# A two-layer diffusion step on one core: P.V by query, one-operation map combination, and early half chunks of the output projection

## What is computed

```python
s = einsum('bqhsd,bkhsd->bshqk', q, k) * scale     # two maps, s = 0, 1
p = softmax(s, axis=-1)
a = p[:, 0] - lam * p[:, 1]
o = einsum('bhqk,bkhe->bqhe', a, v)
o = o * rsqrt(mean(o * o, axis=-1) + 1e-6)         # norm of each query's 128 values of a head
o = o * subln_g * (1.0 - lam_init)
out = concatenate([att, conv], axis=-1) @ w_out
```

## Time and profile before

| | us |
|---|---|
| median of 3 runs | 2104.5 (2101.49 to 2108.45) |
| profiled execution | 2101.44 |
| its span, first to last instruction | 2099.7 |
| PE busy (matmuls) | 1942.6, 93% |
| VectorE busy | 1074.2, 51% |
| ScalarE busy | 811.3, 39% |
| mean granted TensorE clock | 0.959 of 2.4 GHz |

### The profile page before, as it was taken

How to read it: one execution, slowest core, us unless ns; L and a number is a source line. 1 busy time by engine, 2 the same in 40 slices (tenths; PEclk the granted TensorE clock), 3 DMA queues, 4 the chain that set the end, 5 groups by cost and what they waited for, 6 DMA issues and landing times. The chain is left out here.

```text
span 2099.7 us, 29845 instructions
## 1 busy us (share of the span) xinstructions
PE 1942.6 (93%) x12261; PEld 1758.1 (84%) x12261; DVE 1074.2 (51%) x1617; ACT 811.3 (39%) x1316; POOL 114.6 (5%) x93
## 2 busy tenths in 40 slices
PE   5699988989999999989998888699999999999895
PEld 2699956979999999989997578598898998989784
DVE  1542475542322232236326744476676766867574
ACT  3321165242211222233213632465565555655452
POOL 1000000100000000010000001020000000002201
PEclk7899999989999999989999998799999999999997
DMA  8315300322322242304251001366676666768551
GB/s 312 130 72 201 110 1 1 111 85 106 121 73 108 91 177 67 119 31 160 82 201 51 1 11 51 122 219 220 216 243 210 221 220 213 245 210 281 191 179 52
DMA packets 84817, 289.56 MB, mean 138 GB/s; under 512 B 10661, under 2 KB 14117, under 8 KB 84673
## 3 DMA queue, kind: packets, MB, share of 16 engines
q1 hardware_dynamic: 78192, 270.14, 36.9%
q0 software_dynamic: 6480, 17.43, 2.5%
HBM read 281.12 MB, written 12.26 MB: 140 GB/s over the span
## 5 line engine op out<-in xcount | busy, mean ns | idle before, releaser
L1477 DVE TENSOR_TENSOR w_lo<-raw,w_hi 128x1024 fp32r<-128x1024 f32 x396 | 490.6, 1241 | 436.0 <-ACT w_hi L1057 423.2
L1057 ACT ACTIVATE w_hi<-raw 128x1024 fp32r<-128x1024 f32 x396 | 417.2, 1054 | 378.9 <-PE ps L603 179.0
L603 PE MATMUL ps<-a_hi,w_hi 128*128 128x320 f32 x1728 | 403.0, 315 | 30.2 <-DVE w_lo L1477 15.8
L603 PE MATMUL ps<-a_lo,w_hi 128*128 128x320 f32 x1728 | 397.6, 312 | 0.0
L901 PE MATMUL ps<-hg,w_hi 128*128 128x416 f32 x1232 | 386.1, 370 | 12.1 <-DVE w_lo L1477 10.0
L603 PE MATMUL ps<-a_hi,w_lo 128*128 128x320 f32 x1728 | 397.3, 311 | 0.0
L603 PEld LDWEIGHTS ps<-a_hi,w_hi 128*128 128x128 f32 x1728 | 292.2, 191 | 47.6 <-issue 30.6
L902 PE MATMUL ps<-hg,w_lo 128*128 128x208 f32 x1232 | 320.7, 260 | 0.0
L603 PEld LDWEIGHTS ps<-a_lo,w_hi 128*128 128x128 f32 x1728 | 293.2, 190 | 0.0
L603 PEld LDWEIGHTS ps<-a_hi,w_lo 128*128 128x128 f32 x1728 | 292.4, 190 | 0.0
L901 PEld LDWEIGHTS ps<-hg,w_hi 128*128 128x128 f32 x1232 | 234.9, 191 | 15.7 <-DVE w_lo L1477 10.8
(11 more groups left out here) (209 smaller groups left out, 2089.2 us busy)
## 6 DMA issues: line engine op xcount, KB each, us to landing
raw<-gu_w SPq DMA_DIRECT2D x222, 512.0 KB, 4.3
raw<-moe_down_w SPq DMA_DIRECT2D x88, 512.0 KB, 4.4
ada_raw<-ada_w SPq DMA_DIRECT2D x21, 2048.0 KB, 8.0
raw<-in_w SPq DMA_DIRECT2D x48, 512.0 KB, 10.0
raw<-down_w SPq DMA_DIRECT2D x22, 512.0 KB, 3.4
raw<-out_w SPq DMA_DIRECT2D x16, 512.0 KB, 3.5
ada_pro<-ada_w SPq DMA_DIRECT2D x3, 2048.0 KB, 17.6
y_rows<-ey POOLq DMA_DIRECT2D x7, 512.0 KB, 4.1
```

What stands on the lines that cost most here:

```text
L603: ins = nc.tensor.matmul(out[:, hf, 0:HALF], w, o[:, hf * HALF:(hf + 1) * HALF], start=f, stop=e)
L1057: nc.scalar.activation(w_hi[:, s, :], raw[:, n % RAW, :], ACT.Copy).then_inc(hi_done, 1)
L1477: nc.vector.tensor_tensor(w_lo[:, s, :], raw[:, n % RAW, :], w_hi[:, s, :].bitcast(F32), ALU.subtract)\
```

## The change

1. PV by query: the transposed map is the weights, the values move, so an output block has the 128 queries on the partitions and the head's features along the row. VectorE copies it to `att` (`take_output`), at the head of step i for step i-2.
2. Maps combined in one operation: the first map isn't normalised any more. A one-column operation makes `cmix` = -lambda x (row sum 0) / (row sum 1), and one operation makes map 0 + cmix x map 1. The head norm takes the scale out again; its epsilon is multiplied by the square of row sum 0 (`reps`).
3. ScalarE's order in a step: exponential, tail copy, exponential, head copy. Heads 0 to 2 are squared within the steps 7, 12 and 17, and VectorE sums them along the row in steps 8, 13 and 18.
4. The norm per query: sums of squares plus `reps`, root, reciprocal, and a multiplication of each head by its queries' factors (`scale_head`). PE then transposes each head (five blocks) into PSUM blocks 3 and 0 in turn; ScalarE writes the high part with the gain as its scale, VectorE the low part, both from PSUM.
5. The convolution half of output chunk 0 runs in step 19 ahead of its transposes, that of chunk 1 after the last weighing of the values; the head blocks of both follow head by head. Block numbers are padded (`PAD`) so that the two chunks get blocks 1 and 2.
6. The router's small tables move to memory of the expert stage.

```diff
-                 ("sub", 0, 2 * HEADS, 1), ("out", OUT_CH, OUT_CH, OUT_CH), ("norm2", 0, 2, 1)]
+                 ("sub", 0, HEADS, None), ("out", OUT_CH, OUT_CH, OUT_CH), ("norm2", 0, 2, 1)]
...
+            if dg is None:
+
+                dg = (1 - g) % 4
+                PAD[l] = dg
...
-                two_blocks([(n0, g0), (n0 + 1, g0 + 1)], opnd, order, HEADS, KB)
...
-                        ins = nc.tensor.matmul(OT[:, i % 2, :], vtok[:, k0 // P + j, h * VH:(h + 1) * VH],
-                                               pT[:, i % 2, j * P:(j + 1) * P], start=(j == 0), stop=(j == nk // P - 1))
+                        ins = nc.tensor.matmul(OT[:, i % 2, :], pT[:, i % 2, j * P:(j + 1) * P],
+                                               vtok[:, k0 // P + j, h * VH:(h + 1) * VH],
+                                               start=(j == 0), stop=(j == nk // P - 1))
...
+                def first_chunks(cs_, j0, j1):
+
+                    for j in range(j0, j1):
+                        k = order[j]
+                        pe.wait_ge(alo_done, operand[l, "cat"] + j + 1)
+                        for c in cs_:
+                            ins = product(ps[:, (og0 + c) % 4], ((on0 + c) % SPLIT, k), a_hi[:, k, :], a_lo[:, k, :],
+                                          j == 0, j == KB - 1)
+                            if j == KB - 1:
+                                ins.then_inc(mm_done, 1)
...
+                    if i == NS - 1:
+
+                        pe.wait_ge(exp_done, 2 * (l + 1) * NS - 2)
+                        pe.wait_ge(lo_done, on0 + 1)
+                        first_chunks([0], 0, HEADS)
                     pe.wait_ge(comb_done, l * NS + i + 1)
...
                 pe.wait_ge(exp_done, 2 * (l + 1) * NS)
+                pe.wait_ge(lo_done, on0 + 2)
+                first_chunks([1], 0, HEADS)
                 for h in range(HEADS):
-                    pe.wait_ge(att_sq, HEADS * l + h + 1)
-                    sums_of(g0, TT * h, [sq[:, h % 2, :]])
-                    if h % 2:
-                        two_blocks(first, operand[l, "cat"], order, h - 1, h + 1)
-                for h in range(HEADS):
-
-                    pe.wait_ge(att_diag, HEADS * l + h + 1)
+
+                    pe.wait_ge(att_norm, HEADS * l + h + 1)
                     if h >= 2:
-                        pe.wait_ge(att_norm, HEADS * l + h - 1)
-                    spread(g0 + 3 * (h % 2), sq[:, h % 2, :])
+                        pe.wait_ge(alo_done, operand[l, "cat"] + HEADS + h - 1)
+                    flat = ps[:, (3, 0)[h % 2]].rearrange("p b c -> p (b c)")
+                    for t in range(TT):
+                        ins = nc.tensor.transpose(flat[:, t * P:(t + 1) * P], att[:, h, t * P:(t + 1) * P], idn[:])
+                    ins.then_inc(mm_done, 1)
+                    if h:
+                        first_chunks([0, 1], HEADS + h - 1, HEADS + h)
+                first_chunks([0, 1], KB - 1, KB)
...
                 for i in range(NS):
                     exponentials(2 * i)
                     if i >= 1:
+                        take_tail(i - 1)
+                    exponentials(2 * i + 1)
+                    if i >= 1:
                         take_transposed(i - 1)
-                    exponentials(2 * i + 1)
-                    if i >= 2:
-                        take_output(i - 2)
...
+                    if i % 5 == 2 and i > 5:
+                        square_head(i // 5 - 1)
+
+                nc.scalar.activation(warm[:], eps[:], ACT.Sqrt)
+                take_tail(NS - 1)
                 take_transposed(NS - 1)
...
+                square_head(HEADS - 1)
+                act.wait_ge(att_ms, l + 1)
+                nc.scalar.activation(rms[:], ssq[:], ACT.Sqrt, scale=1.0 / VH).then_inc(att_root, 1)
                 for h in range(HEADS):
-                    act.wait_ge(att_norm, HEADS * l + h + 1)
-                    nc.scalar.activation(a_hi[:, h, :], att[:, h, :], ACT.Copy).then_inc(ahi_done, 1)
+                    act.wait_ge(mm_done, q0 + h + 1)
+                    flat = ps[:, (3, 0)[h % 2]].rearrange("p b c -> p (b c)")
+                    nc.scalar.activation(a_hi[:, h, :], flat[:, 0:T], ACT.Copy, scale=subgs[:, l:l + 1])\
+                        .then_inc(ahi_done, 1)
...
+                def take_output(i):
+                    h, t, _, _ = STEPS[i]
+                    dve.wait_ge(pv_done, l * NS + i + 1)
+                    nc.vector.tensor_copy(att[:, h, t * P:(t + 1) * P], OT[:, i % 2, :]).then_inc(att_ready, 1)
+
+                def sum_head(h):
+                    dve.wait_ge(att_sq, HEADS * l + h + 1)
+                    nc.vector.tensor_reduce(ssq[:, h, :], sq[:, h % 2, :].rearrange("p (t c) -> p t c", c=VH), AX, ALU.add)\
+                        .then_inc(att_sum, 1)
...
+                    if i >= 2:
+                        take_output(i - 2)
                     dve.wait_ge(exp_done, 2 * (l * NS + i + 1))
 
-                    link(nc.vector.reciprocal(rinv[:, b, :], rsum[:, b, :]))
-                    link(nc.vector.tensor_scalar(pr[:, b, 1, 0:nk], pr[:, b, 1, 0:nk], rinv[:, b, 1:2], nlam[:, 0:1],
-                                                 ALU.mult, ALU.mult))
-                    nc.vector.scalar_tensor_tensor(pr[:, b, 0, 0:nk], pr[:, b, 0, 0:nk], rinv[:, b, 0:1],
-                                                   pr[:, b, 1, 0:nk], op0=ALU.mult, op1=ALU.add)\
+                    link(nc.vector.reciprocal(rinv[:, b:b + 1], rsum[:, h, t, 1:2]))
+                    link(nc.vector.scalar_tensor_tensor(cmix[:, b:b + 1], rinv[:, b:b + 1], nlam[:, 0:1],
+                                                        rsum[:, h, t, 0:1], op0=ALU.mult, op1=ALU.mult))
+                    nc.vector.scalar_tensor_tensor(pr[:, b, 0, 0:nk], pr[:, b, 1, 0:nk], cmix[:, b:b + 1],
+                                                   pr[:, b, 0, 0:nk], op0=ALU.mult, op1=ALU.add)\
                         .then_inc(comb_done, 1)
...
+                    if i % 5 == 3 and i > 5:
+                        sum_head(i // 5 - 1)
+
+                link(nc.vector.scalar_tensor_tensor(reps[:], rsum[:, :, :, 0], EPS * VH, rsum[:, :, :, 0],
+                                                    op0=ALU.mult, op1=ALU.mult))
+                take_output(NS - 2)
+                take_output(NS - 1)
+                sum_head(HEADS - 1)
+                dve.wait_ge(att_sum, HEADS * (l + 1))
+                nc.vector.tensor_tensor(ssq[:], ssq[:], reps[:], ALU.add).then_inc(att_ms, 1)
...
+                scale_head(0)
+                for h in range(HEADS):
+                    if h + 1 < HEADS:
+                        scale_head(h + 1)
+                    dve.wait_ge(ahi_done, operand[l, "cat"] + HEADS + h + 1)
+                    flat = ps[:, (3, 0)[h % 2]].rearrange("p b c -> p (b c)")
+                    nc.vector.scalar_tensor_tensor(a_lo[:, h, :], flat[:, 0:T], subgs[:, l:l + 1],
+                                                   a_hi[:, h, :].bitcast(F32), op0=ALU.mult, op1=ALU.subtract)\
+                        .then_inc(alo_done, 1)
```

More of the change, by code:

```diff
@@ L190 @@
 DENSE_BLOCKS = blocks_of(DENSE)
+PAD = {}
 def plan():
@@ L285, in hybrid_step @@
         nbias = sb("nbias", [P, 4])
-        rsum = sb("rsum", [P, 2, 2])
-        rinv = sb("rinv", [P, 2, 2])
+        rsum = sb("rsum", [P, HEADS, TT, 2])
+        rinv = sb("rinv", [P, 2])
+        cmix = sb("cmix", [P, 2])
+        ssq = sb("ssq", [P, HEADS, TT])
+        reps = sb("reps", [P, HEADS, TT])
+        warm = sb("warm", [P, 1])
         wr = sb("wr", [P, KB, EXPERTS])
@@ L357, in hybrid_step @@
             ey_lo = sb("ey_lo", [P, ST, D], F32R, c=moe)
+            gates = sb("gates", [P, TT, EXPERTS], c=moe)
+            oh = sb("oh", [P, 2, TT, EXPERTS], c=moe)
+            mask = sb("mask", [P, TT, EXPERTS], c=moe)
+            before = sb("before", [P, TT + 1, EXPERTS], c=moe)
+            rank = sb("rank", [P, TT, EXPERTS + 1], c=moe)
+            grouped = sb("grouped", [P, TT, EXPERTS, 2], F32R, c=moe)
+            logits = sb("logits", [P, TT, EXPERTS], c=moe)
+            tv = sb("tv", [P, TT, 8], c=moe)
+            ti = sb("ti", [P, TT, 8], U32, c=moe)
+            tf = sb("tf", [P, TT, 8], c=moe)
         ht_hi = a_hi[:].rearrange("p a b -> p (a b)").rearrange("p (t d) -> p t d", t=TT)
@@ L391, in hybrid_step @@
         diag_ready = sem("diag_ready")
-        att_diag = sem("att_diag")
+        att_sum = sem("att_sum")
+        att_ms = sem("att_ms")
         xn_done = sem("xn_done")
@@ L770, in turn_weights @@
                     ins.then_inc(done, 1)
+                on0, oq0, og0 = AT[l, "out"]
+                order = [4, 5, 6, 7, 0, 1, 2, 3]
+                def first_chunks(cs_, j0, j1):
[7 more added lines that the diff above has]
+                                ins.then_inc(mm_done, 1)
                 scores(0, 1)
@@ L1180, in take_transposed, with square_head @@
                         .then_inc(pt_ready, 1)
```

(31 more changed lines are left out.)

41 lines of the change are left out of this document (5 added, 36 removed).

## The result

The kernel after takes 2064.93 us (median of 4 runs, 2062.37 to 2067.44) against 2102.99 for the kernel before, measured beside it (2101.31 to 2108.45): ratio 0.9819, 95% interval 0.9804 to 0.9834. That is 38 us less. The forecast was 26 less, and its range ended at 2068: right in sign, too small by 12 us, and outside the range. (Against 2078.5 the miss is 13.6; the other 1.5 is the median of before, 2104.5 when the forecast was made.)

The account below looks back on a forecast made before the run. A loop of waits through three engines bounds the attention step at 4.41 us. Gains of 5.6 + 7.4 = 13.0 a layer, 26 in all, take 2101.4 to 2075.4; the median's 3.1 more gives 2078.5 us, range 2070 to 2086.

Parts of the forecast that it names:

- The loop of the step: Full attention step: PV, output copy on VectorE, reciprocal, small operation, combination, transposes, next PV; 4.30 us, before 4.41.
- PE alone: Full attention step: PE's own work from PV through scores and transposes to the next PV, 4.06 us.
- At PV of step 17: Attention steps up to the start of PV of step 17: 5.6 us per layer saved.
- The end: From the start of PV 17 to the end of output chunks 0 and 1: 25.0 against 32.4, 7.4 us per layer saved.
- The clock: Single stretches at 1.2 GHz: as many as before; none would give back some 5 us, twice as many cost as much.
- rival (d): Attention steps: fuller steps keep the clock up and PE alone bounds them, another 8 us at most, 2070; chance 0.08.
- (6): Shorter PV operands, padded block numbers and small tables placed in the expert stage's memory: counted as nothing.
- (a): Full steps: the output copy holds VectorE's path for 0.6 us, steps take 4.7, time 2088; chance 0.12.
- (b): End of attention: chunk 0's early half delays step 19's transposes, some 2 us a layer, 2082; chance 0.07.
- (c): PV in some 17 steps per layer: exposed weight loads add 0.12 us each, 4 us in all, 2082; chance 0.05.
- (e): Attention steps: head copy behind a late second exponential delays transposes and PV; slower, 2115 at 5.2 a step; chance 0.04.
- (f): In front of output chunk 2: the saved idle time comes back there, so no gain, 2104; chance 0.03.

Follow-up runs that it names:

- filler kernel: The kernel before with matmuls repeated in PE's gaps around the short step, the result unchanged: 2101.1 us, ratio 0.9974 (0.9960 to 0.9988).

## Why the prediction fell short, and what it had right

- **The loop of the step**, forecast 4.30 us, the copy taken at 0.20: measured 4.34 and 0.21. The five gaps of a head were to be 4.44, 4.31, 4.31, 4.05 and 3.40; the trace has 4.42, 4.34, 4.34, 3.95 and 3.40, in all 20.45 for 20.5. That the output copy would be late next, with PE alone right under it, is shown from both sides: twice, it adds 0.33 to a step; away from VectorE, PE alone bounds it. PE alone is 3.99, not 4.06: from scores to transposes 1.49 (1170.10 to 1171.59) where I had taken the idle time off 1.91 and kept 1.56.
- **At PV of step 17**, 5.6 us per layer: from the stage's beginning it took 84.0 us in layer 0 before and 77.3 after, 6.7, of which 1.1 is the one half-clock stretch that went: 5.6.
- **The end**, 7.4 us per layer: from that PV to the end of chunk 1 24.2 us for a forecast 25.0, so 8.2. Most terms are close: up to PV of step 19 7.9 for 8.1, from the head transposes to the first product 2.57 for 2.65, that wait 1.07 within the 1 to 2 named. Most of the 0.8 is in the head products with the transposes between them, 8.44 (353.86 to 362.3) for 7.04 + 1.84, since a set of five transposes holds the products up by 0.46 (355.72 to 356.18) and not by the 0.92 I took.
- Together a stage without clock effects was to give 13.0 and gave 13.9. That is 1.8 us of the miss. In the profiled executions, 39.1 us apart, the miss is 13.1: these 1.8, the clock's 6.3, and 4.9 outside the stages.
- **The clock** is the step that failed: "I take as many as before". Five stretches became none in the stages of after, 6.3 us, about half of the miss. I had seen that PE was busy for 0.83 of 2 us ahead of a fall, and that fuller steps might keep the clock up, but left the gain to rival (d), which I gave 0.08, and let the clock enter the range as 5 us of either sign. It has one sign here. The filler kernel shows the cause for the stretches behind short steps, three of the five: without shortening a step it keeps the clock up. For the two at the end, where the change closes PE's gaps too, the cause is argued. The other kernels fit: five, six and five stretches in the unchanged stages, three and two in those with one edit, none and one in after, one with the output copy elsewhere, and two or three where after is made slower. With 6.3 us more the forecast would have been 2072, inside the range but still high.
- **Outside the stages** another 4.9 us went: 1.3 before, 1.6 between, 2.0 behind. The 2.0 is a second step that failed: (6) put the placing of the small tables at nothing, because no queue gets an instruction. The products of hg cost 0.7 ns less each with the buffers moved, 2.0 us in all. The rest of the span doesn't show it cleanly: 829.0 and 830.3 in the two profiles of before, 827.0 and 826.7 in those of after, but 827.4 with the tables alone and 826.5 to 829.1 in the kernels built on after. The 1.6 is one stretch of 3.4 us fewer (34.1 us at half clock for 37.5). In all fourteen profiles, whatever the edit, the time between the stages goes with the half clock there: 744.2 to 744.3 us at 41.0, 742.6 to 742.8 at 37.5, 741.1 at 34.1, 738.1 and 738.2 at 27.3, 736.8 at 23.9. The kernels on before have 37.5 or 41.0, those on after 23.9 to 41.0; whether the change has a part in that is open. The 1.3 lies within what repeats of one kernel differ by there (262.1 and 263.7).
- **The range** isn't what its terms give: 2 us faster and 7 slower for the copy with 5 either way for the clock are 2071.5 to 2090.5, not 2070 to 2086.
- **The rivals.** (a), the dear copy, fell: it holds VectorE 0.21 us (0.33 when the next instruction is linked to it). (b) fell: the early half is worth 1.6 a layer. (c) fell: weight loads of PV start with the tail copy as before, and from transposes to PV it is 0.98 (280.12 to 281.10), before 0.97. So did (e): no head copy holds the transposes up, and heads are shorter. (f) fell. (d) was half right: the clock, not PE alone.
- **The rule of the Trainium skill** ("TensorE: Matmul & The Clock Gate", Part 2) that weight loads are pulled ahead of running matmuls would have made (c) cost 4 us. In the traces the operands' exchange cost nothing, and in before the load of the values, long in memory, also came only with the tail copy: no run here shows a load pulled ahead across that wait.

## What to carry to other kernels

Where three engines stand in a loop, cut all links that an edit shortens and add those that it closes: here two edits worth 1.7 and 1.3 us a head alone gave 1.4 together, because a copy of 0.2 us moved onto the engine in the middle; putting it back on ScalarE gave 0.9 more, and then PE alone was the bound. Where a granted clock of 0.5 stands behind PE's gaps, count it as part of the price of those gaps, with a sign: a change that fills them gets it back, and one that opens them pays again. Where buffers move, take a repeated product's busy time into account: 0.7 ns by 2816 products was 2 us. Before a step's order is tuned, compute the time of PE alone, which tells what is left (3.99 of 4.34 here).

## What was not expected of the hardware

- Redundant matmuls made a kernel faster: 36 more (72 records), 5 us less (0.9974).
- Of the five falls of the clock in the stages of before, three come behind the gap of PE at a short step (292, 1166 and 1211 us), one behind the gap at the end (1225), and one 3.4 us after that one has ended. All five are 3.4 us long. One costs 1.0 to 1.2 us in the full steps of before (5.44 to 5.65 for 4.41), and 1.4 to 1.6 between the stages, where PE is busy for 98% of the time.
- One stretch of the repeated kernel with the copy on ScalarE lasted 10.2 us in layer 0 and made that stage 2.9 us longer (115.8 against 112.9 in layer 1), with the same instructions.
- The same products cost PE 151.8 ns each in one kernel and 151.0 in one that differs only in where buffers lie.
